# HGRN2 and Fourier block on one core: scores in three visits a step, far operands in buffers of their own, some products in two column parts

## What is computed

```python
def chunk_scan(q, k, v, log_f, s0):          # per head, chunks of 32 tokens
    bcum = jnp.cumsum(gc, axis=2)
    o_inter = jnp.einsum("bhtd,bhde->bhte", qc * jnp.exp(bcum), state)
    scores = jnp.einsum("bhtd,bhsd,bhtsd->bhts", qc, kc, decay)   # decay = exp(bcum_t - bcum_s), s <= t
    o_intra = jnp.einsum("bhts,bhse->bhte", scores, vc)
    state = state * jnp.exp(b_end)[:, :, 0, :, None] + jnp.einsum("bhsd,bhse->bhde", kc * jnp.exp(b_end - bcum), vc)
...
i_in, z_f, z_b, q_in, gate_a, u_f, gate_f = split_proj(h @ w_in)
o = chunk_scan(q, k_f, v, g_f, s0_f) + flip(chunk_scan(flip(q), flip(k_b), flip(v), flip(g_b), s0_b))
y_a = rmsnorm_per_head(o) * silu(gate_a);  y_f = fourier_mix(u_f) * silu(gate_f)
out = concatenate([y_a, y_f]) @ w_out
```

## Time and profile before

| | us |
|---|---|
| median of 3 runs | 2189.35 (2189.27 to 2191.93) |
| profiled execution | 2188.86 |
| its span, first to last instruction | 2187.0 |
| head stage, near of the first step to near of the last | 515.8 to 1653.8 |
| step of ten halves, g = 0 and 1 / g = 2 and 3 | 36.8 / 38.6 to 38.7 |

### The profile page before, as it was taken

How to read it: one execution, slowest core, us unless ns; L and a number is a source line. 1 busy time by engine, 2 the same in 40 slices (tenths; PEclk the granted TensorE clock), 3 DMA queues, 4 the chain that set the end, 5 groups by cost and what they waited for, 6 DMA issues and landing times.

```text
span 2187.0 us, 48218 instructions
## 1 busy us (share of the span) xinstructions
PE 2113.0 (97%) x20564; PEld 1777.1 (81%) x20564; DVE 1531.4 (70%) x3275; ACT 507.7 (23%) x836; POOL 74.9 (3%) x109
## 2 busy tenths in 40 slices
PE   5899999999999999999999999999997999999997
PEld 3799988788888888888888888878776887888886
DVE  5865855016877878778778878788988886555554
ACT  3711134111112111212111121112113343222121
POOL 0000101000000000000000000000000010000000
PEclk9899999999999999999999999999998999999999
DMA  8434645332424234342434243343235466535451
GB/s 316 163 122 142 195 150 155 131 127 74 132 88 133 93 101 130 96 130 94 125 97 132 86 125 104 91 131 122 91 113 190 156 235 236 186 125 171 142 180 56
DMA packets 229863, 298.89 MB, mean 137 GB/s; under 512 B 14934, under 2 KB 159990, under 8 KB 226322
## 3 DMA queue, kind: packets, MB, share of 16 engines
q1 hardware_dynamic: 145346, 178.38, 25.2%
q10 hardware_dynamic: 73952, 81.18, 11.0%
q0 software_dynamic: 10352, 36.25, 5.1%
HBM read 198.16 MB, written 97.59 MB: 135 GB/s over the span
## 4 chain that ended last, share of the span: by engine, by line
PE 90%; DVE 4%; DMA 2%; ACT 1%; SPq 1%; issue 1%; ACTq 0%; DVEq 0%
PE all_bank L61 26%; PE all_bank L63 24%; PE all_bank L62 24%; PE all_bank L1511 3%; PE all_bank L1314 3%; PE all_bank L1465 2%; PE all_bank L1481 2%; PE all_bank L1494 2%; PE all_bank L1504 1%; PE all_bank L1313 1%; DVE hidden_h_lo L483 1%; DMA front_w_mod<-in_w_ada 1%; SPq L366 1%; PE all_bank L1008 1%; PE all_bank L2594 1%
## 5 line engine op out<-in xcount | busy, mean ns | idle before, releaser
L61 PE MATMUL all_bank<-hidden_h_hi,head_hi 128*128 128x512 f32 x1184 | 491.0, 415 | 1.3 <-issue 1.3
L63 PE MATMUL all_bank<-hidden_h_hi,head_lo 128*128 128x512 f32 x1184 | 465.6, 393 | 0.0
L62 PE MATMUL all_bank<-hidden_h_lo,head_hi 128*128 128x512 f32 x1184 | 463.4, 391 | 0.0
L1550 ACT ACTIVATE head_projected<-all_bank 128x512 f32<-128x512 f32 x148 | 88.4, 597 | 865.8 <-PE all_bank L63 865.8
L63 PEld LDWEIGHTS all_bank<-hidden_h_hi,head_lo 128*128 128x128 f32 x1184 | 222.6, 188 | 51.9
L61 PEld LDWEIGHTS all_bank<-hidden_h_hi,head_hi 128*128 128x128 f32 x1184 | 222.8, 188 | 48.2 <-issue 3.0
L62 PEld LDWEIGHTS all_bank<-hidden_h_lo,head_hi 128*128 128x128 f32 x1184 | 223.4, 189 | 40.9 <-issue 1.2
L1640 DVE RECIPROCAL head_inverse<-head_gate 128x448 f32<-128x448 f32 x64 | 185.0, 2924 | 0.0
L1691 DVE TENSOR_TENSOR head_query<-head_query,head_total 128x256 f32<-128x256 f32 x256 | 107.7, 421 | 82.0 <-PE all_bank L1481 52.0
L61 PE MATMUL all_bank<-front_hi,hidden_h_hi 128*128 128x256 f32 x512 | 143.9, 281 | 0.0
L63 PE MATMUL all_bank<-front_hi,hidden_h_lo 128*128 128x256 f32 x512 | 142.8, 279 | 0.0
(11 more groups left out here) (294 smaller groups left out, 4144.1 us busy)
## 6 DMA issues: line engine op xcount, KB each, us to landing
head_raw<-in_w_in POOLq DMA_DIRECT2D x37, 512.0 KB, 4.8
head_value<-value_rows SPq DMA_DIRECT2D x64, 256.0 KB, 5.1
head_query<-piece_query SPq DMA_DIRECT2D x64, 256.0 KB, 6.8
head_out<-head_o ACTq DMA_DIRECT2D x64, 256.0 KB, 5.9
tail_o<-head_out SPq DMA_DIRECT2D x32, 512.0 KB, 5.9
front_raw<-in_w_in SPq DMA_DIRECT2D x19, 512.0 KB, 5.1
front_stage<-in_x SPq DMA_DIRECT2D x16, 512.0 KB, 6.7
front_w_mod<-in_w_ada SPq DMA_DIRECT2D x8, 1024.0 KB, 13.5
```

The source lines that it names most:

```text
L61: nc.tensor.matmul(out, st_hi, mv_hi, start=start, stop=False)
L62: nc.tensor.matmul(out, st_hi, mv_lo, start=False, stop=False)
L63: return nc.tensor.matmul(out, st_lo, mv_hi, start=False, stop=stop)
L1550: nc.scalar.activation(projected[unit % 2][:], ps_proj[unit % 2][:], PIECES[name][1], scale=PIECES[name][2]).then_inc(proj_copied, 1)
```

## The change

1. The far operands get buffers of their own: `query_planes` and `key_planes`, two planes of 512 columns each, "far" and "turned". Key and query are now single buffers; the key is loaded first, on its own semaphore `key_here`, once near product and far operand of the step are through. One score buffer moves, to make room.
2. `far_operands` stands at the end of a step, behind the next step's `first_operands`; at a head's end `split_low` stands between the two.
3. TensorE makes near and level 0 in one visit, level 1 in a second, level 2 and level 3 in a third. For level 3 each 64x64 block is four-fold in the array: 32 executed products with 32 rows and 64 columns, whose halves come from both planes (`joint_key`, `joint_query`). Level 2's operands are written out of place, so VectorE makes levels 1 and 2 (index i = 1, 2 of `next_level`) one after the other without waiting for a product between.
4. ScalarE copies the quarter that level 3 left in the turned plane back to the far plane (semaphore `returned`, four copies of 128 elements a step), for which the transposes wait.
5. `mm3_by_columns` makes the products for k > 0 in two parts of 256 columns, in the front's last four units and in listed numbers of k in the heads (`BY_COLUMNS`: 22 in step 0 of most heads, that is 66 products).

```diff
+def mm3_by_columns(nc, out, st_hi, st_lo, mv_hi, mv_lo, stop):
+    n = out.shape[-1]
+    for st, mv in ((st_hi, mv_hi), (st_hi, mv_lo), (st_lo, mv_hi)):
+        for cols in (slice(0, n // 2), slice(n // 2, n)):
+            last = nc.tensor.matmul(out[:, cols], st, mv[:, cols], start=False, stop=stop and st is st_lo and cols.stop == n)
+    return last
...
+                if k and unit >= 2 * NG:
+                    last = mm3_by_columns(nc, *operands, k == KT - 1)
...
+    BY_COLUMNS = {(0, 0): 20, **{(h, 0): 22 for h in range(1, HEADS - 1)}, (HEADS - 2, 1): 10, (HEADS - 2, 2): 15,
+                  (HEADS - 1, 0): 22, (HEADS - 1, 1): 22, (HEADS - 1, 2): 10}
...
+    query_far = [query_planes[d][:, d, :] for d in range(2)]
+    key_far = [key_planes[d][:, 1 - d, :] for d in range(2)]
+    query_turned = [query_planes[d][:, 1 - d, :] for d in range(2)]
+    key_turned = [key_planes[d][:, d, :] for d in range(2)]
...
+                    if after is not None:
+                        wait_count(sp, product[d], PROD * after + 1)
+                        wait_count(sp, operand[d], OPS * after + 2)
+                    sp.dma_start(key[d][:], scratch[key_names[d]][bass.ds(h * P, P), t:t + GRP]).then_inc(key_here[d], DMA)
...
-            project_half(h, g, 1)
-            project_half(h, g, 2)
...
+            level_in_parts(n, 0)
+            for slot in range(1, 3):
+                project_half(h, g, slot)
+            level_in_parts(n, 1)
+            for slot in range(3, 5):
+                project_half(h, g, slot)
+            for d in range(2):
+                wait_count(pe, operand[d], OPS * n + 4)
...
+                        done = nc.tensor.matmul(ps[d][2][PARTS[s], t, PARTS[q]], tile(key_far[d], t)[:, PARTS[s]], tile(query_far[d], t)[:, PARTS[q]],
+                                                start=True, stop=True)
...
+            for d in range(2):
+                wait_count(pe, operand[d], OPS * n + 5)
+            for t in range(TPG):
+                for side in range(2):
+                    for d in range(2):
+                        done = nc.tensor.matmul(ps[d][2][PARTS[2 * d + side], t, (1 - d) * 64:(2 - d) * 64], joint_key(d)[:, 2 * t + d, side, :],
+                                                joint_query(d)[:, 2 * t + 1 - d, :, :], start=True, stop=True)
...
+            for slot in range(5, 8):
+                project_half(h, g, slot)
...
+                wait_count(pe, returned[d], 2 * (n + 1))
...
+        def far_operands(h, g):
+            n = NG * h + g
+            for d in range(2):
+                qs, ks, q_far, k_far, f = (in_blocks(ap, d) for ap in (query[d][:], key[d][:], query_far[d], key_far[d], gate[d][:]))
+                wait_count(v, product[d], PROD * n)
+                wait_count(v, operand[d], OPS * n + 1)
+                nc.vector.tensor_tensor(q_far, qs, f[:, :, 0:1].to_broadcast([P, GRP // BASE, BASE]), ALU.mult)
...
             for d in range(2):
+                next_level(n, d, 0)
...
+            prepare_next(1, (0, 1))
+            for i in (1, 2):
                 for d in range(2):
+                    next_level(n, d, i)
+            prepare_next(2, (2, 3))
+            prepare_next(3, (4, 5))
+            for d in range(2):
+                next_level(n, d, 3)
+            prepare_next(4, (6, 7))
...
+            if not ends:
+                first_operands(*next_step(h, g))
             if g == NG - 1 and not last:
                 split_low(h + 1, 0)
             if not ends:
-                first_operands(*next_step(h, g))
+                far_operands(*next_step(h, g))
```

More of the change, by code:

```diff
@@ L1414, in turn @@
                 start_state(h)
-            for g in range(0 if h else 1, NG):
+            for g in range(NG):
                 if g == NG - 1 and last:
                     break
-                for d in range(2):
-                    wait_count(sp, product[d], PROD * (NG * h + g))
                 if g < NG - 1:
-                    load(h, g + 1)
+                    load(h, g + 1, after=NG * h + g)
                 else:
@@ L1433, in _ @@
     def _(pe):
+        by_columns = {(h, g): BY_COLUMNS.get((h, g), 0) for h in range(HEADS) for g in range(NG)}
         def project_half(h, g, slot):
@@ L1463, in step @@
                     for part in PARTS:
-                        for half, keys in enumerate((first_half[d], key[d][b])):
+                        for half, keys in enumerate((first_half[d], key[d])):
                             done = nc.tensor.matmul(half_block(ps[d][0][part, t, part], d, half), tile(keys, t)[:, part],
-                                                    half_block(tile(query[d][b], t)[:, part], d, half), start=True, stop=True)
+                                                    half_block(tile(query[d], t)[:, part], d, half), start=True, stop=True)
@@ new lines, in step @@
+            for d in range(2):
+                wait_count(pe, operand[d], OPS * n + 5)
+            for t in range(TPG):
+                for side in range(2):
+                    for d in range(2):
+                        done = nc.tensor.matmul(ps[d][2][PARTS[2 * d + side], t, (1 - d) * 64:(2 - d) * 64], joint_key(d)[:, 2 * t + d, side, :],
+                                                joint_query(d)[:, 2 * t + 1 - d, :, :], start=True, stop=True)
+                        if t == TPG - 1 and side == 1:
+                            done.then_inc(product[d], 1)
@@ L1559, in step @@
             n = NG * h + g
-            for slot in range(9):
+            for slot in range(5):
+                evacuate(h, g, slot)
+            for d in range(2):
+                wait_count(act, product[d], PROD * n + 5)
+                for into, turned, two in ((key_far[d], joint_key(d), 1 - d), (query_far[d], joint_query(d), d)):
+                    a = 1 - two
+                    into, turned = (ap.rearrange("p (n two) a c -> p n two a c", two=2)[:, :, two, a, :] for ap in (blocks_of_32(into), turned))
+                    nc.scalar.activation(into, turned, ACT.Copy).then_inc(returned[d], 1)
+            for slot in range(5, 9):
                 evacuate(h, g, slot)
@@ L1674, in step, with prepare_next @@
                 v.wait_ge(handed.masks_in, DMA)
+            def prepare_next(level, parts):
+                due = split_due(h, g, level)
+                if not ends:
+                    prepare(*next_step(h, g), parts[0])
+                if due is not None:
+                    split_low(h, due)
+                if not ends:
+                    prepare(*next_step(h, g), parts[1])
             for d in range(2):
+                next_level(n, d, 0)
+            for d in range(2):
+                wait_count(v, product[d], PROD * n + 1)
                 if g < NG // 2:
```

184 lines of the change are left out of this document (100 added, 84 removed).

## The result

| | us |
|---|---|
| before, median of 3 | 2189.35 |
| the change, median of 3 | 2167.35 (2166.41 to 2170.96) |
| ratio | 0.9908, 95% interval 0.9892 to 0.9923 |
| forecast | 2164.5, range 2150 to 2183 |

The change is faster by 1%, as forecast. Two more sets of runs beside the experiments gave 2165.87 and 2166.48, ratios 0.9902 (0.9889 to 0.9915) and 0.9901 (0.9888 to 0.9915).

What follows compares the result with a forecast made beforehand. TensorE, busy 97% of the span, was taken to bound the kernel, except in the last two heads. Terms of -20.9, +3, +1.7, -9.5, +3 and -2 summed to -24.7 us, giving a median of 2,164.5 us, range 2,150 to 2,183.

Steps and rivals of the forecast that it cites:

- Term 1: Merged visits of small products: level 0 behind near -0.30 us, level 3 behind level 2 -0.37, in 31 steps: -20.9 us.
- Term 2: 777 products in two parts of 256 columns, 84 in the front, 693 in the heads: -2.7 to +6.8 us, taken as +3.
- Term 3: VectorE's moved work: far operands fit before near, but the later weight split stalls TensorE 0.25 us seven times: +1.7 us.
- Term 4: Heads 6 and 7: four TensorE gaps, read as missing instructions, go, -9.5 us; VectorE's late chain is charged +3 (0 to 9).
- the count of packet ends: Heads 6 and 7: ends of 256-instruction packets fall 150 to 237 instructions into merged near and level 0, except in one step.
- Term 5: Last step, without projections: two of TensorE's waits for VectorE merge or go, against a later delivery: -2 us.
- the one that the count is off: Merged visit: instructions run out if packet ends are miscounted by 60 or more; 2,261 us at 2.8 us in 31 steps; 9%.

Runs made afterwards that it cites:

- the shifted run: The changed kernel with head 0's 60 products whole instead of in column parts, so all later TensorE instructions stand 120 places earlier: 2247.03 us, 1.0258 of before.

## Why the prediction was right

The sum of the terms was -24.7 us; the medians are 22.0 apart, the spans 22.4. Each term against the traces:

- **Term 1** (-20.9 in 31 steps, -0.67 each): measured -0.32 and -0.34, -0.66 a step. The guess of 14 ns for level 3's new form was 15. The two merged visits are most of the change's gain: taken apart in 24 steps they cost 6.7 and 9.7 us by the medians, 7.7 and 8.6 by the profiled executions.
- **Term 2** (+3): parts start 117 to 118 ns apart in most heads, 113 in head 3 and 114 in head 5, against 230 for a whole product. A ten-half step with them (60 products in head 0, 66 in the others) takes 36.4 to 36.5 us in four of six heads, 36.1 and 36.2 in two, against 36.11. That is 1.6 us in heads 0 to 5. In the last two heads gaps stand in the same steps; at 5 ns a product their 303 would cost 1.5 us, an estimate from the distances.
- **Term 3** (+1.7 for the split): 1.7. The rest was covered as argued.
- **Term 4** (-9.5 for the gaps, +3 for VectorE): the mechanism is shown, and the count of packet ends held. But two gaps of 1.2 and 1.1 us (distance of starts) stayed in head 7, in steps with ends 16 (with 272) and 237 places in, and one of 0.4 in head 6; I had called all but one place safe. What the count of ends inside the merged visit missed is the next packet. It ends in level 1, 528 and 493 places in, and slot 2 is empty in heads 6 and 7, so with one half in it it was used up in 4.0 to 4.1 us, while its successor's transfer started only 2.8 and 2.3 us after its beginning, took 0.95 and 1.5, and work went on 1.5 and 1.4 behind that. And VectorE was not late at all, so its charge of 3 was wrong. The two errors, 2.4 us of gaps that stayed and 3 us that were not needed, cancel: that this term came out is in part luck.
- **Term 5** (-2): -1.2, for all behind the last near product; the two other traces of the change, 530.5 and 533.7 us, put it between -2.7 and +0.4. A gap of 3.7 us at a packet end now stands where VectorE was waited for.

Sum by the trace: -13.1 in heads 0 to 5, -10.3 in heads 6 and 7, -1.2 behind them, +2.2 of scatter ahead of them, -22.4. Of the rivals, the one that the count is off was no mishap far away: with everything 120 places earlier the change is 59 us slower than the kernel before, not faster. Its price of 87 us for 31 gaps of 2.8 was near the 80 of 24 gaps with their low clock.

## What to carry to other kernels

Small products that follow big ones cost some 0.3 us for each visit, by both mergings measured here: put them together, and let the operands stand in buffers of their own so that they can. Count instructions as well as time: where some hundred short ones follow each other, a packet end among them, or one shortly behind them, can stop the engine for 2 us and halve its clock for 3 more, so gaps that the profile puts down to nothing should be looked up against multiples of 256, and an edit's time should not be believed before its shift of the later instructions is known. Idle time of an engine is room only for work that doesn't wait for the same thing.

## What was not expected of the hardware

- Sixty products more or less, far from the place, moved the kernel by 80 us.
- After a gap of about 2 us TensorE was granted 1.2 GHz for some 3 us in most cases, 17 of 24 in the shifted run, but not after all: step 0 of heads 2 and 5 of the shifted run, with gaps of 2.8 and 2.5 us, took 38.9 and 39.0 us, the gap alone.
- Products of 256 columns start 113 to 114 ns apart in some heads and 118 in others, with the same operands in name. In three traces of the same kernel head 2 has 118, 113 and 118, and head 4 has 118, 114 and 114, so it is not fixed by the program. What decides it was not tried.
